# Seven block products in place of eight in the last two panels of an output projection

## The chip, the core and the metric

One core of a Trainium2 chip runs the whole kernel. The metric is the device time of one execution in microseconds (us); the time before is the median of three runs.

## The reference, cut to what matters

One layer of a decoder works on 512 prompt rows and 32 sample rows, 544 in all, of width 1024. After two gated branches come the output projection, a channel mixer and an embedding:

```python
merged = jax.nn.sigmoid(gate_a) * (a @ w_oa) + jax.nn.sigmoid(gate_b) * (b @ w_ob)
x = x + merged @ w_o
h2 = _rmsnorm(x, g_ffn)
x = x + jnp.square(jax.nn.relu(h2 @ w_ff1)) @ w_ff2
gate = jax.nn.sigmoid(_rmsnorm(x, g_ple) @ w_ple_gate)
x = x + gate * (pe @ w_ple_proj)
```

The change concerns `merged @ w_o`, a product of 544x1024 with 1024x1024 in float32.

## The kernel before, in words

**Precision.** Every float32 operand is split into a rounded part (`..._hi`, type fp32r, cast by ScalarE) and the rest (`..._lo`, a subtraction by VectorE). A product is three matmuls: hi with hi, hi with lo, lo with hi.

**Layout.** Activations lie transposed: 8 blocks of 128 features, each with 544 columns, used as two halves of 272. The merged activation is `mA`; half of it is split into `h_hi` and `h_lo`. The residual stream is `xT`.

**Panels and units.** Weights come in panels of 256 columns (512 KB in each of two loads), and each panel gives two units of 128 output features. In the first part of the kernel a *slot* is one unit; each engine's program is written out slot by slot, with its work for a slot in a fixed order (the loops over `SLOTS`, TensorE L1581, VectorE L2042, ScalarE L1078, GpSimd L2389). The projection is the kind `wo`, four panels, units 0 to 7, slots 96 to 103; the branch's `ob` ends in slot 95, and eight short units `pj` (the ple projection, 12 matmuls each) follow in slots 104 to 111. A `wo` unit is 48 matmuls: 8 blocks of the inner dimension, three matmuls, two halves (`block_unit`, L1336).

**What a `wo` slot does before.** ScalarE casts the next panel (`split_hi`, L749), evacuates the unit (`evacuate`, L825) and squares the new `xT` block for the norm (`square_x`, L924). VectorE splits the next panel (`split_lo`, L1704) and adds the unit to `xT` (`add_to_x`, L1959). GpSimd adds the square to `ss` (`add_square`, L2372). Slots 96 to 98 also take transposes of the ple input (`take_transposes`, L938). The SP queue loads each panel once the panel before it in the same buffer is split (`load_panel`, L621).

**Seven products.** The channel mixer already has panels (`seven`, L115) that multiply 2x2 blocks by seven products in place of eight. Weights and activation are cut in 2x2 blocks: the inner dimension into 512 and 512, the two units of the panel, and the two halves of the columns. A product (`product`, L1599) is 12 matmuls of 272 columns: 4 blocks, three matmuls. The order is p1, p2, p5, p6, p4, p3, p7 (`PRODUCTS`, L127). Four combinations of the activation are summed by VectorE (`combine`, L1768), cast by ScalarE (`combined_hi`, L1190) and subtracted by VectorE (`combined_lo`, L1781). The combinations of the weights are four in-place sums of 128x512 blocks by VectorE (`add_blocks`, L1731), each after the one before, then cast (`sums_hi`, L780) and split (`pair_lo`, L1717). A half-width block is split apart (`one_hi`, L772; `one_lo`, L1724). Four partial results are copied from the accumulator (`part`, L785) and added (`add_parts`, L1741). A panel has four counts of finished weight splits, which TensorE waits for before p1, p2, p5 and p6. Split weights lie in four places of 1024 columns, taken in turn; a cast waits for the last product that read the place (`pair_hi`, L762).

**The norm after the projection.** `ss` is complete after the eighth square; TensorE sums it after `pj` unit 3 (`norm_sum`, L1538), VectorE and GpSimd make the inverse root (`norm_mean`, L1962; `norm_inverse`, L2384), and TensorE spreads it inside the first unit of the channel mixer (`norm_spread`, L1545).

## Time and profile before

| what | value |
|---|---|
| time, median of 3 runs | 1044.94 us |
| lowest and highest run | 1041.84 and 1045.57 us |
| profiled execution: span | 1041.0 us |
| profiled execution: its own time outside the span | not given |
| TensorE matmuls, busy | 1023.5 us, 98% |
| VectorE busy | 774.4 us, 74% |
| ScalarE busy | 518.5 us, 50% |
| GpSimd busy | 245.6 us, 24% |
| projection `wo` in the trace | 547 to 596.7 us |

How to read it: the span runs from the first to the last instruction of one execution. The busy share of matmuls counts pipelined instructions whose ends are modelled. Times in the rows below are microseconds from the span's start; "PE" is TensorE, "PEld" its weight loads, "DVE" VectorE, "ACT" ScalarE, "POOL" GpSimd. In lists in order of time, a bracket gives the idle time of the engine before the instruction and what ended it.

### The profile page before, as it was taken

How to read it: one execution, taken by the hardware profiler on the slowest of the kernel's cores; microseconds unless marked ns; L12 is line 12 of the kernel's file. 1: busy time of each engine (PE TensorE's matmuls, PEld its weight loads, DVE VectorE, ACT ScalarE, POOL GpSimd, SP SyncE). 2: the span in 40 equal slices, each digit the busy share in tenths (PEclk: the TensorE clock that was granted, in tenths of full speed). 3: DMA queues.
4: the chain of work that ended last, by engine and by line, in shares of the span. 5: the costliest groups of instructions: out<-in, count | busy, mean ns of one | idle time of the engine just before them, and what ended most of it. 6: DMA issues, size and time to landing. Idle time of an engine off the chain costs nothing.

```text
span 1041.0 us, 20872 instructions
## 1 busy us (share of the span) xinstructions
PE 1023.5 (98%) x8310; PEld 1008.5 (97%) x8310; DVE 774.4 (74%) x1004; ACT 518.5 (50%) x1253; POOL 245.6 (24%) x381
## 2 busy tenths in 40 slices
PE   9999999999999999999999999999999999999997
PEld 7999999999999999999999989999999999999997
DVE  6679888988899878999674368747856875786553
ACT  6773797658845574352264385414522531453332
POOL 2441233122312003958201211100100100012300
PEclk9999999999999999999999999999999999999999
DMA  6557556776687765776843335655664574573412
GB/s 186 192 178 231 200 177 208 227 242 206 208 256 213 210 218 148 224 218 186 258 142 122 122 122 208 214 183 172 229 209 152 195 247 168 171 252 130 162 54 86
DMA packets 131634, 195.89 MB, mean 188 GB/s; under 512 B 32321, under 2 KB 109473, under 8 KB 129746
## 3 DMA queue, kind: packets, MB, share of 16 engines
q1 hardware_dynamic: 107616, 125.51, 37.9%
q0 software_dynamic: 10560, 63.28, 18.3%
q10 hardware_dynamic: 13362, 5.77, 2.0%
q8 instruction: 66, 1.08, 0.4%
q14 instruction: 30, 0.25, 0.1%
HBM read 185.55 MB, written 62.00 MB: 238 GB/s over the span
## 4 chain that ended last, share of the span: by engine, by line
PE 66%; DVE 13%; ACT 5%; issue 5%; DMA 5%; POOL 3%; SPq 3%; ACTq 0%; DVEq 0%; POOLq 0%
PE gm L1347 26%; PE gm L1603 7%; PE psSO L1603 4%; PE gm L1321 4%; PE gm L1322 3%; PE gm L1323 3%; PE psT L1603 3%; DMA w_raw<-in_w_in 3%; PE psSO L1651 2%; PE psSO L1347 2%; PE psT L1347 2%; PE psT L1651 2%; DVE w_lo L1708 2%; POOL kv L2363 2%; ACT prob L1123 2%
## 5 line engine op out<-in xcount | busy, mean ns | idle before, releaser
L1321 PE MATMUL gm<-w_hi,h_hi 128*128 128x256 f32 x640 | 186.9, 292 | 1.1 <-DVE w_lo L1708 0.9
L1322 PE MATMUL gm<-w_hi,h_lo 128*128 128x256 f32 x640 | 180.8, 282 | 0.0
L1323 PE MATMUL gm<-w_lo,h_hi 128*128 128x256 f32 x640 | 180.1, 281 | 0.0
L1347 PE MATMUL gm<-h_hi,w_hi 128*128 128x272 f32 x624 | 132.7, 294 | 0.4 <-ACT z L852 0.4
L1347 PE MATMUL gm<-h_hi,w_lo 128*128 128x272 f32 x624 | 130.0, 290 | 0.0
L1347 PE MATMUL gm<-h_lo,w_hi 128*128 128x272 f32 x624 | 129.4, 289 | 0.0
L1321 PEld LDWEIGHTS gm<-w_hi,h_hi 128*128 128x128 f32 x640 | 120.8, 189 | 3.1 <-issue 1.7
L1323 PEld LDWEIGHTS gm<-w_lo,h_hi 128*128 128x128 f32 x640 | 121.2, 189 | 0.0
L1322 PEld LDWEIGHTS gm<-w_hi,h_lo 128*128 128x128 f32 x640 | 120.6, 188 | 0.0
L2352 POOL DMA_DIRECT2D out_kvs<-in_cache_kv_w x64 | 35.0, 547 | 345.2 <-PE gm L1347 120.6
L1708 DVE TENSOR_TENSOR w_lo<-w_raw,w_hi 128x1024 fp32r<-128x1024 f32 x76 | 90.5, 1228 | 21.3 <-ACT w_hi L755 20.8
L1347 PEld LDWEIGHTS gm<-h_hi,w_hi 128*128 128x128 f32 x624 | 98.1, 190 | 1.5 <-ACT z L852 0.6
L1347 PEld LDWEIGHTS gm<-h_lo,w_hi 128*128 128x128 f32 x624 | 98.6, 190 | 0.0
L1347 PEld LDWEIGHTS gm<-h_hi,w_lo 128*128 128x128 f32 x624 | 98.2, 190 | 0.0
L755 ACT CAST w_hi<-w_raw 128x1024 fp32r<-128x1024 f32 x76 | 76.8, 1046 | 30.4 <-DMA w_raw<-in_w_in 16.5
L765 ACT CAST w_hi<-w_raw 128x1024 fp32r<-128x1024 f32 x49 | 50.2, 1048 | 82.6 <-PE psSO L1347 28.5
L1347 PE MATMUL gm<-x_hi,w_hi 128*128 128x272 f32 x384 | 80.4, 291 | 0.0
L1347 PE MATMUL gm<-x_hi,w_lo 128*128 128x272 f32 x384 | 79.6, 289 | 0.0
L1347 PE MATMUL gm<-x_lo,w_hi 128*128 128x272 f32 x384 | 79.3, 288 | 0.0
L2363 POOL DMA_DIRECT2D kv<-in_cache_kv_w x128 | 69.4, 708 | 32.8 <-DVE acc L1954 16.8
L1721 DVE TENSOR_TENSOR w_lo<-w_raw,w_hi 128x1024 fp32r<-128x1024 f32 x49 | 59.0, 1221 | 11.9 <-ACT w_hi L765 11.8
L1347 PEld LDWEIGHTS gm<-x_lo,w_hi 128*128 128x128 f32 x384 | 60.4, 189 | 0.0
(378 smaller groups left out, 2662.7 us busy)
## 6 DMA issues: line engine op xcount, KB each, us to landing
out_kvs<-in_cache_kv_w POOLq DMA_DIRECT2D x64, 510.0 KB, 4.7
w_raw<-in_w_in SPq DMA_DIRECT2D x60, 512.0 KB, 6.2
w_raw<-in_w_ff SPq DMA_DIRECT2D x36, 512.0 KB, 5.7
kv<-in_cache_kv_w SPq DMA_DIRECT2D x128, 128.0 KB
kv<-in_cache_kv_w SPq DMA_DIRECT2D x64, 256.0 KB
out_kvs<-in_cache_kv_w POOLq DMA_DIRECT2D x32, 508.0 KB, 5.3
w_more<-in_w_ff SPq DMA_DIRECT2D x26, 512.0 KB, 6.1
kv<-in_cache_kv_w POOLq DMA_DIRECT2D x128, 64.0 KB, 3.3
```

Source lines behind the costliest of these rows:

```text
L755: nc.scalar.copy(w_hi[:, r, hh * 1024:(hh + 1) * 1024], w_raw[:, hh]).then_inc(w_hi_done, 1)
L765: nc.scalar.copy(w_pair(w_hi, PAIRS[p] + n).rearrange("p (k n) -> p k n", k=4), raw(p, hh)).then_inc(w_hi_done, 1)
L1321: nc.tensor.matmul(out, lh, wh, start=k == 0, stop=False)
L1322: nc.tensor.matmul(out, ll, wh, start=False, stop=False)
L1323: last = nc.tensor.matmul(out, lh, wl, start=False, stop=k == KD - 1)
L1347: last = nc.tensor.matmul(pair[:, half, 0:HALF], w, x[:, k0 + k, half * HALF:(half + 1) * HALF], start=first, stop=end)
L1603: last = nc.tensor.matmul(bank[:, 0:HALF], w[wx][:, k], x[xx][:, k], start=start and k == 0 and wx == xx, stop=k == 3 and wx == 1, skip_gr ...
L1651: last = nc.tensor.matmul(banks(u + sub)[:, half, 0:HALF], w, x[:, k, half * HALF:(half + 1) * HALF], start=first, stop=end, skip_group_ch ...
L1708: vec.tensor_tensor(w_lo[:, r, cols], w_raw[:, hh], w_hi[:, r, cols].bitcast(F32), ALU.subtract).then_inc(w_lo_done, 1)
L1721: vec.tensor_tensor(w_pair(w_lo, x).rearrange("p (k n) -> p k n", k=4), raw(p, hh), w_pair(w_hi, x).rearrange("p (k n) -> p k n", k=4).bit ...
L2352: pool.dma_start(dst, src).then_inc(cache_copied, 16)
L2363: pool.dma_start(dst, src).then_inc(late_landed[n % RING], 16)
```

## The change

Panels 2 and 3 of `wo` (`MIXED`, units 4 to 7) become seven-product panels. Their activation combinations are taken from `mA`, in slots 96 to 98, beside units 0 to 2 (`combine_mixed` and `mixed_lo` on VectorE, `mixed_hi` on ScalarE, with the factor 0.5 in the last two). They lie in new tiles `tc_hi` and `tc_lo` over inputs of the earlier projections. Panel 2's weight sums are made in slots 98 and 99, panel 3's in slot 100; panel 3 is loaded into a new buffer `w_mixed` over the first part of `mA`, once the four sums are made. The units are added to `xT` by `add_to_mixed`. Panel 2 accumulates in `psT` and `psSO`, panel 3 in `gm`. The squares of units 4 to 7 go to `sqf`. Counts of semaphores of the channel mixer are shifted to match. `pair_free`, `product` and `seven_products` move up in the file. The first weights of the channel mixer are cast in `pj` slots 0 and 3, after the evacuation, where the first cast stood in the last `wo` slot. The diff, cut:

```diff
+MIXED = [PANELS.index(("wo", 0, i)) for i in (2, 3)]
+
+
 def seven(p):
 
     j, q = divmod(p - P_FF, FF_PANELS)
-    return P_FF <= p < P_PG and q < 4 and (j > 0 or q >= 2)
-
-
-SEVENS = [p for p in range(P_FF, P_PG) if seven(p)]
+    return p in MIXED or P_FF <= p < P_PG and q < 4 and (j > 0 or q >= 2)
+
+
+SEVENS = [p for p in range(P_PG) if seven(p)]
+
+
+def first_unit(p):
+
+    return UNIT["wo", 2 * PANELS[p][2]] if p in MIXED else U_FF + 2 * (p - P_FF)
...
     j, q = divmod(p - P_FF, FF_PANELS)
+    if p == MIXED[1]:
+        return 3
...
     p = P_FF + (u - U_FF) // 2
+    if u < U_FF:
+        return (2 if UNITS[u][0] == MIXED[0] else 0) + u % 2
...
+        w_mixed = sb("w_mixed", [128, 2, 1024], F32, A_QK1)
+        tc_hi = [sb(f"tc_hi{x}", [128, 4, HALF], F32R, A_QK + x * XB) for x in range(4)]
+        tc_lo = [sb(f"tc_lo{x}", [128, 4, HALF], F32R, A_V + x * XB) for x in range(4)]
+        wo_one_hi = sb("wo_one_hi", [128, 2, 512], F32R, A_R + 4 * NT * 4)
+        wo_one_lo = sb("wo_one_lo", [128, 2, 512], F32R, A_R + 4 * NT * 4 + 4096)
...
+                    w_mixed[:, hh].rearrange("p (k n) -> p k n", k=4))[raw_set(p)]
+
+        def one_place(p):
+
+            n = SEVENS.index(p) % 2
+            hi, lo = (wo_one_hi, wo_one_lo) if p in MIXED else (w_one_hi, w_one_lo)
+            return [x[:, n].rearrange("p (k n) -> p k n", k=4) for x in (hi, lo)]
 
         def w_pair(hi, n):
 
...
+                        sp.wait_ge(xc_summed, 8)
                     nk = 1024 // (256 if p >= P_FF else COLS.get(PANELS[p][0], 256))
-                    dst = raw(p, hh) if p >= P_FF else w_raw[:, hh].rearrange("p (k n) -> p k n", k=nk)
...
+                    act.wait_ge(ss_done, 4)
+                u = first_unit(p)
                 src = banks(u + 1)[:, 1, 0:HALF] if bank else banks(u)[:, 1, 0:HALF]
                 nc.scalar.copy(dst, src).then_inc(part_out, 1)
...
+            def mixed_hi(n):
+
+                x, src, scale = ((2, 0, 0.5), (0, 1, 0.5), (1, 1, -0.5), (3, 1, 0.5))[n]
+                act.wait_ge(xc_summed, n + 1)
+                nc.scalar.mul(tc_hi[x][:], xc_sum[src][:], scale).then_inc(xc_hi_done, 1)
+
+            def mixed_slot(s):
+
+                p = UNITS[s][0]
+                if s == first_unit(MIXED[0]):
+                    sums_hi(p, 0, 2)
+                    one_hi(p + 1)
+                    part(p, 0)
+                    raw_hi(p + 1, 1)
+                    part(p, 1)
+                    part(p, 2)
+                elif s == first_unit(MIXED[0]) + 1:
+                    sums_hi(p + 1, 1, 1)
+                    part(p, 3)
+                    square_x(4, 4, zc(UNIT["wo", 4]))
+                elif s == first_unit(MIXED[1]):
+                    sums_hi(p, 0, 2)
+                    square_x(5, 5, zc(UNIT["wo", 5]))
+                    part(p, 0)
+                    raw_hi(p + 1, 0)
+                    part(p, 1)
+                    part(p, 2)
+                else:
+                    raw_hi(p + 1, 1)
+                    part(p, 3)
+                    square_x(6, 6, zc(UNIT["wo", 6]))
+                    square_x(7, 7, zc(UNIT["wo", 7]))
 
             def gained_hi(n, m, zu):
...
                 p, kind, g, i, sub = UNITS[s]
+                if p in MIXED:
+                    mixed_slot(s)
+                    continue
...
+                    one_hi(MIXED[0])
+                    raw_hi(MIXED[0], 1)
+                    mixed_hi(3)
+                elif sub == 0 and not late_split(s) and kind != "pj":
                     split_hi(p + 1, (p + 1) % 2, panel_end(p - 1))
+                if s == UNIT["wo", 3]:
+                    sums_hi(MIXED[0], 1, 1)
                 if s - 1 in MERGED:
                     merged_hi(MERGED[s - 1])
+                if s == UNIT["wo", 0]:
+                    mixed_hi(0)
+                    mixed_hi(1)
+                if s == UNIT["wo", 1]:
+                    mixed_hi(2)
                 if s >= 1 and UNITS[s - 1][4] == 2 and UNITS[s - 1][1] == "v":
                     act.wait_ge(unit_out, s)
                 evacuate(s)
                 if late_split(s):
                     split_hi(p + 1, (p + 1) % 2, panel_end(p - 1) if p >= 1 else None)
-                if (kind, i, sub) == ("wo", 3, 1):
-                    half_hi(P_FF, 0)
-                if (kind, sub) == ("pj", 3):
-                    half_hi(P_FF, 1)
+                if kind == "pj" and sub in (0, 3):
+                    raw_hi(P_FF, sub // 3)
                 if kind == "pj":
                     if sub == 0:
-                        act.wait_ge(unit_ready, READY[UNIT["wo", 7]])
...
                         last = block_unit(r, n, 128 * sub, 2, b2, pT_hi, pT_lo, split=split)
+
+            def pair_free(u):
+
+                if UNITS[min(u, U_FF - 1)][0] == MIXED[0]:
+                    pe.wait_ge(o_out, len(PIECES))
+                    pe.wait_ge(t_out, TINDEX[("ps",)] + 1)
+                elif u < U_FF:
+                    pe.wait_ge(unit_out, u - 3)
+                elif pair_before(u) is not None:
+                    pe.wait_ge(unit_out, pair_before(u) + 1)
...
+                pair_free(u + 1)
+                product(p, "p1", B, one, x11, True)
+                pe.wait_ge(w_lo_done, SPLITS[p] + 2)
+                pair_free(u)
+                product(p, "p2", A, bd[0], x21, True)
+                pe.wait_ge(w_lo_done, SPLITS[p] + 3)
+                if n in (0, len(MIXED)):
+                    pe.wait_ge(xc_lo_done, 4 if n == 0 else 8)
+                product(p, "p5", C, yu[1], t1, True)
+                pe.wait_ge(w_lo_done, SPLITS[p] + 4)
+                pe.wait_ge(part_out, 4 * n + 1)
+                product(p, "p6", B, wv[0], t2, False)
+                product(p, "p4", Dd, bd[1], t4, True)
+                pe.wait_ge(part_out, 4 * n + 2)
+                product(p, "p3", C, yu[0], x22, False)
+                pe.wait_ge(part_out, 4 * n + 3)
+                product(p, "p7", B, wv[1], t3, False)
 
...
+                if UNITS[s][0] in MIXED:
+                    if UNITS[s][4] == 0:
+                        seven_products(UNITS[s][0])
+                    continue
...
                 j, uu = divmod(2 * (p - P_FF) + m, FF_UNITS)
-                if uu >= 2:
+                if p in MIXED:
+                    dve.wait_ge(z_used, zc(first_unit(p)) - 1 + (m if p == MIXED[1] else 0))
+                elif uu >= 2:
...
                 vec.tensor_tensor(x2_lo[:, uu], z[:, m], x2_hi[:, uu].bitcast(F32), ALU.subtract).then_inc(hid_lo, 1)
+
+            def add_to_mixed(p, m):
+
+                dve.wait_ge(unit_out, first_unit(p) + m + 1)
+                x = xT[:, 2 * PANELS[p][2] + m]
+                vec.tensor_tensor(x, x, z[:, m], (ALU.add, ALU.subtract)[m]).then_inc(z_used, 1)
+
+            def mixed_slot(s):
+
+                p = UNITS[s][0]
+                if s == first_unit(MIXED[0]):
+                    pair_lo(p, 0, 2)
+                    one_lo(p + 1)
+                    pair_lo(p + 1, 1, 0)
+                    for n in range(4):
+                        add_blocks(p + 1, n)
+                elif s == first_unit(MIXED[0]) + 1:
+                    add_parts(p, 0)
+                    pair_lo(p + 1, 1, 1)
+                    add_to_mixed(p, 0)
+                    add_parts(p, 1)
+                    add_to_mixed(p, 1)
+                elif s == first_unit(MIXED[1]):
+                    pair_lo(p, 0, 2)
+                    pair_lo(p + 1, 0, 0)
+                else:
+                    add_parts(p, 0)
+                    pair_lo(p + 1, 1, 1)
+                    add_to_mixed(p, 0)
+                    add_parts(p, 1)
+                    add_to_mixed(p, 1)
+
+            def combine_mixed(n):
+
+                first, second = slice(0, HALF), slice(HALF, NT)
+                top, low = mA[:, 0:4], mA[:, 4:8]
+                out, in0, in1, op = ((0, low[:, :, second], top[:, :, second], ALU.subtract),
+                                     (1, top[:, :, first], top[:, :, second], ALU.subtract),
+                                     (1, xc_sum[1][:], low[:, :, second], ALU.add),
+                                     (1, xc_sum[1][:], low[:, :, first], ALU.subtract))[n]
+                dve.wait_ge(z_used, zc(UNIT["ob", 7]))
+                if n >= 2:
+                    dve.wait_ge(xc_summed, n)
+                    dve.wait_ge(xc_hi_done, n)
+                vec.tensor_tensor(xc_sum[out][:], in0, in1, op).then_inc(xc_summed, 1)
+
+            def mixed_lo(n):
+
+                x, src, scale = ((2, 0, 0.5), (0, 1, 0.5), (1, 1, -0.5), (3, 1, 0.5))[n]
+                dve.wait_ge(xc_summed, n + 1)
+                dve.wait_ge(xc_hi_done, n + 1)
+                vec.scalar_tensor_tensor(out=tc_lo[x][:], in0=xc_sum[src][:], scalar=scale, in1=tc_hi[x][:].bitcast(F32), op0=ALU.mult,
+                                         op1=ALU.subtract).then_inc(xc_lo_done, 1)
 
             def combine(n):
...
+                if p in MIXED:
+                    mixed_slot(s)
+                    continue
...
-                if sub == 0 and not late_split(s) and kind != "pj":
+                if s == UNIT["wo", 2]:
+                    one_lo(MIXED[0])
+                    pair_lo(MIXED[0], 1, 0)
+                    mixed_lo(3)
+                    add_blocks(MIXED[0], 0)
+                    add_blocks(MIXED[0], 1)
+                elif sub == 0 and not late_split(s) and kind != "pj":
                     split_lo(p + 1, (p + 1) % 2)
+                if s == UNIT["wo", 3]:
+                    add_blocks(MIXED[0], 2)
+                    add_blocks(MIXED[0], 3)
+                    pair_lo(MIXED[0], 1, 1)
                 if kind == "pj" and sub in (0, 5):
-                    half_lo(P_FF, sub // 5)
+                    pair_lo(P_FF, sub // 5, sub // 5)
                 if s == 63:
...
+                if s == UNIT["wo", 0]:
+                    combine_mixed(0)
+                    combine_mixed(1)
+                    mixed_lo(0)
+                    mixed_lo(1)
+                if s == UNIT["wo", 1]:
+                    combine_mixed(2)
+                    mixed_lo(2)
+                    combine_mixed(3)
                 if kind == "ob":
                     m, r = 4 * i + sub, (zc(s) - 1) % 2
...
                     pool.wait_ge(ss_done, n)
-                    gp.tensor_tensor(ss[:], ss[:], sq[:, m % 2], ALU.add).then_inc(ss_done, 1)
+                    gp.tensor_tensor(ss[:], ss[:], (sqf if 4 <= n < KD else sq)[:, m % 2], ALU.add).then_inc(ss_done, 1)
 
...
```

## Rows read from the trace of the kernel before

**Rows 1.** The page: the span, and each engine's busy time.
```profile
span 1041.0 us, 20872 instructions
...
PE 1023.5 (98%) x8310; PEld 1008.5 (97%) x8310; DVE 774.4 (74%) x1004; ACT 518.5 (50%) x1253; POOL 245.6 (24%) x381
```

**Rows 2.** The chain of waits: start, us, engine, tile, line.
```profile
569.40 27.27 PE gm L1347 x216
...
612.97 1.13 PE psSO L1548 x2
...
719.01 10.57 PE gm L1603 x84
```

**Rows 3.** Windows: us, busy PE, PEld, DVE, ACT, POOL, clock, DMA.
```profile
572.00:584.00 12.00, 12.00 (x98) 12.00 (x97) 4.28 (x5) 4.44 (x6) 3.18 (x3) 1.00 0.41 141
```

**Rows 4.** Source lines: ns min/median/max, first and last start, shapes.
```profile
L1779 DVE TENSOR_TENSOR xc_sum<-x_gain,x_gain x1: 1293/1293/1293, 619.6 to 619.6; 128x1088 f32<-128x1088 f32 x1
...
L1196 ACT ACTIVATE xc_hi<-xc_sum x4: 1114/1114/1116, 620.9 to 637.1; 128x1088 fp32r<-128x1088 f32 x4
...
L1786 DVE SCALAR_TENSOR_TENSOR xc_lo<-xc_sum,xc_hi x4: 1282/1284/1292, 625.7 to 638.3; 128x1088 fp32r<-128x1088 f32 x4
...
L1739 DVE TENSOR_TENSOR w_raw<-w_raw x28: 682/691/694, 631.8 to 908.8; 128x512 f32<-128x512 f32 x28
...
L1721 DVE TENSOR_TENSOR w_lo<-w_raw,w_hi x49: 1212/1220/1227, 616.2 to 1012.4; 128x1024 fp32r<-128x1024 f32 x49
...
L765 ACT CAST w_hi<-w_raw x49: 1032/1050/1055, 611.9 to 1011.1; 128x1024 fp32r<-128x1024 f32 x49
```

**Rows 5.** Order of time: VectorE, then ScalarE, in the output projection.
```profile
548.75 2.36 DVE L1708 TENSOR_TENSOR w_lo<-w_raw,w_hi 128x1024 fp32r<-128x1024 f32 x2
551.03 0.72 DVE L2151 SCALAR_TENSOR_TENSOR h_lo<-mA,h_hi 128x544 fp32r<-128x544 f32 x1
554.00 0.72 DVE L1960 TENSOR_TENSOR xT<-xT,z 128x544 f32<-128x544 f32 x1 [2.25 <-ACT z L895]
...
572.63 0.61 ACT L895 COPY z<-gm 128x544 f32<-128x544 f32 x1 [2.87 <-PE gm L1347]
```

**Rows 6.** VectorE beside GpSimd: order of time, and one source line.
```profile
574.78 1.36 POOL L2382 TENSOR_TENSOR ss<-ss,sq 128x544 f32<-128x544 f32 x1 [3.96 <-ACT sq L929]
...
575.67 2.69 DVE L1708 TENSOR_TENSOR w_lo<-w_raw,w_hi 128x1024 fp32r<-128x1024 f32 x2 [1.53 <-ACT w_hi L755]
...
L1983 DVE SCALAR_TENSOR_TENSOR h_lo<-xT,gcol,h_hi x16: 761/779/1347, 601.2 to 982.6; 128x544 fp32r<-128x544 f32 x16
...
555.54 0.63 POOL L2379 COPY ss<-sq 128x544 f32<-128x544 f32 x1 [19.12 <-ACT sq L929]
...
944.39 0.72 DVE L1960 TENSOR_TENSOR xT<-xT,z 128x544 f32<-128x544 f32 x1
...
944.43 1.18 POOL L2379 COPY ss<-sq 128x544 f32<-128x544 f32 x1 [11.61 <-ACT sq L929]
```

**Rows 7.** Order of time: VectorE, GpSimd, ScalarE round the projection's end.
```profile
579.29 0.73 DVE L1960 TENSOR_TENSOR xT<-xT,z 128x544 f32<-128x544 f32 x1 [0.93 <-ACT z L895]
...
580.80 1.35 POOL L2382 TENSOR_TENSOR ss<-ss,sq 128x544 f32<-128x544 f32 x1 [4.18 <-ACT sq L929]
...
599.60 0.60 ACT L892 COPY proj<-gm 128x544 f32<-128x544 f32 x1
```

**Rows 8.** TensorE in order of time, and windows of 1 us.
```profile
513.18 1.05 PE L1464 MATMUL psT<-fold,acc 128*128 128x32 f32 x8 [1.52 <-DVE acc L2128]
...
515.00:516.00 1.00, 1.00 (x8) 1.00 (x7) 0.03 (x1) 0.00 (x0) 0.00 (x0) 0.64 0.78 307
516.00:517.00 1.00, 1.00 (x6) 1.00 (x6) 0.00 (x0) 0.00 (x0) 0.00 (x0) 0.50 1.07 340
...
518.00:519.00 1.00, 1.00 (x7) 1.00 (x7) 0.00 (x0) 0.12 (x1) 0.00 (x0) 0.65 1.00 293
...
600.25 0.52 PE L1347 MATMUL gm<-pT_hi,w_hi 128*128 128x272 f32 x2 [0.60 <-ACT proj L892]
```

More of the change, by code:

```diff
@@ L1386, in unit, with product @@
                         last = block_unit(r, n, 128 * sub, 2, b2, pT_hi, pT_lo, split=split)
+            def pair_free(u):
[6 more added lines that the diff above has]
+                    pe.wait_ge(unit_out, pair_before(u) + 1)
+            def product(p, name, bank, w, x, start):
+                for k in range(4):
+                    for wx, xx in ((0, 0), (0, 1), (1, 0)):
+                        last = nc.tensor.matmul(bank[:, 0:HALF], w[wx][:, k], x[xx][:, k], start=start and k == 0 and wx == xx,
+                                                stop=k == 3 and wx == 1, skip_group_check=True)
+                last.then_inc(unit_ready, 1)
@@ new lines, in seven_products @@
+            def seven_products(p):
+                n, u, s = SEVENS.index(p), first_unit(p), PAIRS[p]
+                (A, C), (Dd, B) = (banks(u)[:, 0], banks(u)[:, 1]), (banks(u + 1)[:, 0], banks(u + 1)[:, 1])
+                one = one_place(p)
+                bd, yu, wv = [[[block_of(w_pair(x, s + y), m) for x in (w_hi, w_lo)] for m in range(2)] for y in range(3)]
+                first, second = slice(0, HALF), slice(HALF, NT)
+                x11, x21, x22 = [[x[:, k:k + 4, cols] for x in (h_hi, h_lo)] for k, cols in ((0, first), (4, first), (4, second))]
+                t1, t2, t3, t4 = [[tc_hi[x], tc_lo[x]] if p in MIXED else [xc_hi[x], xc_lo[x]] for x in range(4)]
+                pe.wait_ge(w_lo_done, SPLITS[p] + 1)
+                pair_free(u + 1)
[15 more added lines that the diff above has]
+                product(p, "p7", B, wv[1], t3, False)
@@ L2029, in _ @@
                 tile_half_lo(0, half)
-                half_lo(0, half)
+                first_lo(half)
             tile_lo(1)
```

97 lines of the change are left out of this document (31 added, 66 removed).

## The prediction, made before the change was run

> **What bounds the kernel now.** I read the page first, for the engines' shares: TensorE is busy 98% of a span of 1041.0 us [rows 1], so only TensorE time counts, and other engines matter where TensorE waits for them. Next the chain of waits round the change: from 569.40 to 596.67 it is TensorE alone, then ScalarE and VectorE take most of it until the spread of the norm at 612.97, inside the first unit of the channel mixer [rows 2]. Then the windows: in the second half of the output projection VectorE and ScalarE are busy under 4.5 of 12 us [rows 3], so the change moves work to engines with room on average. Whether it is on time is a matter of order, so the last views are the lists in order of time.
>
> The profiled span stands 3.9 us below the median of 1044.94, and 0.8 below the fastest run. No view shows more of that execution than its span. The sum below is a difference; I carry it over to the median.
>
> **What is taken away.** A panel of two units has 96 matmuls, seven products of 12 have 84. In the channel mixer 84 of these take 10.57 us [rows 2], 0.126 each; 24 fewer are worth **3.0 us**. The casts, splits and evacuations that go with them were off the path.
>
> **What is added, and when it is done.** Four sums of the merged activation, four halved casts, four differences; per panel one half-width split, one more full split, four sums of weight blocks, four evacuated parts and two adds into z. All have like-shaped rows [rows 4]: 1.29 a sum, 1.11 a cast, 1.28 a difference, 0.69 a block sum, 1.22 and 1.05 a weight split on VectorE and ScalarE; the parts are half as wide as an evacuation, and an add is 0.73 [rows 7]. Between dependent instructions of two engines I put 0.04 us; one that follows on its own engine with no dependence starts 0.07 to 0.09 before the other ends. The starting point is unchanged: VectorE's last piece of h_lo at 551.03 [rows 5].
>
> Sums 0 and 1 then end at 552.95 and 554.16, ScalarE's casts at 554.10 and 555.31, the differences at 556.64. The add of unit 0 into xT starts at 556.6 where it was 554.00, and its evacuation, which now stands behind two casts, ends 2.0 us later. Nothing waits: unit 2 needs that bank at 559.7. The next slot, by the same steps, ends the fourth sum at 562.51; that frees the SP queue to load the last panel, 15 us before ScalarE wants it. Behind it in SP's queue stands the load of the ple projection, which waits for panel 2's last split, at 580.0 below, and is wanted some 10 us after. Behind GpSimd's adds stand copies of the cache, which no engine here waits for.
>
> In the third slot ScalarE does the half block (565.35), the other half (566.30), the fourth cast (567.33) and only then evacuates unit 2 (567.84, 1.1 late). VectorE follows with two splits, the last difference (568.78), two block sums (570.12), the add of unit 2 (570.76) and a split of pT (571.36). The transposes of the ple input are taken at 571.7, just before panel 2 needs their bank at 572.45.
>
> Then it gets late. VectorE has two block sums left. The square of unit 2 ends at 571.46, and GpSimd adds it. **A VectorE instruction with two SBUF inputs that meets such an add is held up**: a pair of splits that meets 0.47 us of it takes 2.69 [rows 6], not 2.36 [rows 5], and of 16 pieces of h_lo one takes 1.35 where the median is 0.78 [rows 6]. The other way round GpSimd waits: its copy takes 1.18 where VectorE was first, 0.63 alone [rows 6]. So the third block sum holds GpSimd off until 571.97, the fourth waits for GpSimd and ends at 573.8 in place of 572.7. By the Trainium skill (SBUF — State Buffer, Who interferes with whom) this is an exclusive lock, held for the whole instruction, and the loser blocks. The pair lost 0.33 of its 0.47, and I take 0.14 off each overlap; by the full overlap the total below would be some 0.5 us higher.
>
> ScalarE casts the first summed block from 573.84 to 574.89, then evacuates unit 3 (575.4; PE had ended it at 572.45). VectorE splits that block until 576.15 and adds unit 3 to xT until 576.80; ScalarE squares it (577.5) and casts the second summed block until 578.45. VectorE's split of that meets 0.44 us of GpSimd's add and ends at 580.0.
>
> TensorE in panel 2: p1 and p2 run 572.45 to 575.46. p5 needs the split of 576.15: **0.74 us lost**. p6 needs that of 580.0: **2.36 lost**. p4, p3 and p7 follow to 586.08.
>
> Panel 3: its first sums end at 584.54 and the split for p5 at 586.9, early. The add of unit 4 ends at 587.53, that of unit 5 gets the port first and holds GpSimd's add of square 4 back to 588.9 to 590.15. The second sum's split, ready at 589.2, meets this and ends at 591.25, when p6 has waited since 590.6: **0.7 lost**. p7 ends at **597.3**, where the last unit ended about 596.5.
>
> The ple projection: before, its first evacuation starts at 599.60 [rows 7], after an evacuation, an add, a square and a cast. Now ScalarE has square 6 and square 7 in front. The add of unit 6 ends at 598.34; GpSimd's add of its square starts 1.51 us after that add's start (579.29 to 580.80 in [rows 7]), at 599.12, and VectorE's add of unit 7, two dependent instructions after the same start, at 599.13. If GpSimd is first, unit 7 ends at 600.9, if VectorE is, at 599.85. The bounds are 0 and 1.1 us; I take GpSimd, by the 0.01 that the rows give it. Square 7 ends at 601.6, the first evacuation at 602.1; the cast of the mixer's first weights, which stood ahead of it, now stands behind, and costs TensorE's second pair of banks 0.3. From there the order of before leads to the spread of the norm at 615.2, where it was 612.97 [rows 2].
>
> **Sum:** -3.0 for matmuls, +3.8 for three waits, +1.4 before the norm: **+2.2 us**, 1047.1. Of the 1.4, 1.1 hang on the near tie. Later panels only shift: they keep the order of their queues, the weights' buffers and the count of sums.
>
> Bounds of what no row shows: whether the block sums meet GpSimd's adds. Never: 1.1 less in panel 2, 0.7 in panel 3, 1.1 at the tie, which leaves -0.7, 1044.2. Fully, by overlap: +2.7, 1047.6.
>
> **Rivals.**
> *The cover holds.* If evacuation and square of unit 3 come a microsecond or two earlier than my twenty-step chain, p5 and p6 wait under 0.5 us each, and the tie falls to VectorE: -3.0, +1.0 for waits, +0.3: 1043.2, or 1042.3 with no waits at all. For it: VectorE and ScalarE have over 7 of 12 us free [rows 3]. Against: each step waits for the other engine, so the free time can't be used.
> *The clock falls.* After 511.4 TensorE idled 1.52 us and ran eight narrow transposing matmuls, and the granted clock went to 0.50, its lower level of 1.2 GHz, from about 515 to 519 [rows 8]. Lost there, by four windows of 1 us, the middle two alike: 0.36 + 0.50 + 0.50 + 0.35 = 1.7 us. Panel 2's waits of 0.74 and 2.36 us, with one product between them, are like it: +1.7, 1048.8. Against: 0.60 us of idleness in the ple projection left the matmuls after it at full pace [rows 8]. The Trainium skill (TensorE: Matmul & The Clock Gate, What's actually happening) says "the default state is throttled, and activity releases the throttle"; by that rule the long wait would count against the change, while here one stretch shows it.
> *Slower by more than 0.5%.* The same fall, but lasting, because p6 of panel 3 and the ple projection wait too. At 1.2 GHz work takes twice its time; it decides once 24 matmuls (3.0 us at full clock) more than forecast have run at the lower level, 6 us of it against 3.5 in [rows 8]. At 7.5 us: +2.2 +3.8, 1050.9. Against: at half clock the products are long enough for the splits to be on time, so the waits that would hold it down vanish.
> *The change does less than it says*: no sign; the products are the same helper as in the mixer.
>
> **How the numbers follow.** Forecast (1045.5 to 1048.2) 0.43; cover holds 0.24 (1042.3 to 1044.5); clock falls 0.22; lasting fall 0.09; anything else 0.02. A measurement of this kernel can tell about 0.5%, 5.2 us: 1039.7 to 1050.2. The removed work is 3.0 us, so faster by more needs a low median besides (runs of before differ by 3.7): 0.03. Slower: the lasting fall, and a clock fall on a high median: 0.11. Same: 0.86. The range takes the cover's 1042.3 less 0.5 and the clock's 1048.8 plus 1.0.
>
> **What would show it.** 24 fewer matmuls in the projection's panels; TensorE waits for w_lo before p5 and p6 of panel 2 (0.7 and 2.4) and p6 of panel 3 (0.7); VectorE's block sums and splits stretched beside ss adds; the first proj evacuation some 2 us later; granted clock 1.00 from 572 to 600. If p6 waits under 1 us, or the span of the projection shrinks by 2 us or more, my chain is wrong; a clock of 0.5 there speaks for the third case.

## The result, and the profile after

Run beside each other, the changed kernel took 1045.55 us (median of 22 runs) and the kernel before 1042.60 (22 runs): ratio 1.0026, 95% interval 1.0013 to 1.0038, so 2.7 us slower (1.4 to 4.0). A second series of 7 runs gave 1.0043 (1.0028 to 1.0059), 4.5 us. Both ratios lie within the 0.5% that the prediction called no change, on the slower side.

The first part of the profile's page after:

```profile
span 1043.1 us, 20886 instructions
...
PE 1021.9 (98%) x8286; PEld 1006.0 (96%) x8286; DVE 798.4 (77%) x1028; ACT 525.8 (50%) x1265; POOL 245.6 (24%) x381
```

Against [rows 1] TensorE has the 24 matmuls fewer and 1.6 us less to do, and the span is 2.1 us longer. VectorE has 24.0 us more, ScalarE 7.3: they are still far from full. The loss must be waits, so the list to read is TensorE in order of time, with the idle time and its releaser in brackets at the end:

```profile
574.09 0.40 PE L1474 MATMUL psT<-tc_hi,w_hi 128*128 128x272 f32 x1 [0.55 <-DVE w_lo L1801]
577.91 0.60 PE L1474 MATMUL psSO<-tc_hi,w_hi 128*128 128x272 f32 x1 [2.05 <-DVE w_lo L1801]
...
590.43 0.39 PE L1474 MATMUL gm<-tc_hi,w_hi 128*128 128x272 f32 x1 [0.25 <-DVE w_lo L1801]
598.67 0.52 PE L1419 MATMUL gm<-pT_hi,w_hi 128*128 128x272 f32 x2 [0.41 <-DVE z L1833]
...
601.70 0.52 PE L1419 MATMUL gm<-pT_hi,w_hi 128*128 128x272 f32 x2 [1.26 <-ACT proj L917]
603.80 0.52 PE L1419 MATMUL gm<-pT_hi,w_hi 128*128 128x272 f32 x2 [0.34 <-ACT proj L917]
...
615.03 1.12 PE L1666 MATMUL psSO<-sqf,ones 128*128 128x512 f32 x2 [0.80 <-DVE sqf L2105]
```

The first three are p5 and p6 of the first of the two panels and p6 of the second, waiting for VectorE's half of a weight split; the next three are the ple projection. Before, the same stretch had one such wait, 0.60 us in the ple projection [rows 8], beside the 0.80 at the spread of the norm, which both kernels have:

```profile
596.49 0.41 PE L1347 MATMUL gm<-pT_hi,w_hi 128*128 128x272 f32 x2
...
612.97 1.13 PE L1548 MATMUL psSO<-sqf,ones 128*128 128x512 f32 x2 [0.80 <-DVE sqf L1971]
```

The window that was full of TensorE work before [rows 3] reads after the change:

```profile
572.00:584.00 12.00, 9.40 (x62) 8.96 (x61) 8.03 (x10) 6.45 (x10) 1.79 (x2) 0.86 0.51 173
```

Two numbers in it: TensorE idle for 2.6 of 12 us, and a granted clock of 0.86.

**How to compare these profiles.** The profile after can't be set beside that of before by its clock time: its last piece of h_lo, up to which the two kernels do the same work, starts at 548.93, where it was 551.03 [rows 5].

```profile
548.93 0.71 DVE L2298 SCALAR_TENSOR_TENSOR h_lo<-mA,h_hi 128x544 fp32r<-128x544 f32 x1
```

So I cut every profile of this study, those of the experiments below included, at two events that all kernels have: the start of that piece of h_lo, and TensorE's start of the spread of the norm (612.97 before [rows 2]). The stage between them holds the whole change. Medians and ratios are from the timed runs, the other columns from the one profiled execution of each kernel, in us:

| kernel | median, ratio to before in its series | h_lo | spread | stage | spread to end |
|---|---|---|---|---|---|
| before | 1042.60 | 551.03 | 612.97 | 61.94 | 428.0 |
| less24 | 1038.88, 0.9963 | 549.75 | 608.72 | 58.97 | 428.2 |
| changed | 1045.55, 1.0026 | 548.93 | 615.03 | 66.10 | 428.1 |
| after_again | 1046.24, 1.0043 | 550.18 | 615.09 | 64.91 | 428.0 |
| filled_wait | 1046.32, 1.0031 | 551.81 | 616.76 | 64.95 | 428.0 |
| early_splits | 1045.13, 1.0017 | 556.34 | 620.46 | 64.12 | 428.0 |
| short_gpsimd | 1042.09, 0.9990 | 550.79 | 612.54 | 61.75 | 428.0 |
| squares_behind | 1043.64, 1.0017 | 545.88 | 609.59 | 63.71 | 428.0 |
| early_parts | 1042.31, 1.0003 | 549.51 | 612.31 | 62.80 | 428.0 |
| early_parts_and_squares | 1040.75, 0.9989 | 548.04 | 609.62 | 61.58 | 428.0 |
| all_parts_first | 1042.62, 1.0003 | 559.39 | 620.60 | 61.21 | 428.0 |
| all_parts_short_gpsimd | 1040.79, 0.9983 | 549.58 | 609.99 | 60.41 | 428.2 |
| both_again | 1042.55, 0.9993 | 552.23 | 613.79 | 61.56 | 428.2 |
| all_parts_again | 1041.23, 0.9984 | 556.11 | 616.92 | 60.81 | 428.1 |

The last column is the same in all fourteen to 0.2 us: whatever the stage loses, the end loses, and nothing is given back or lost behind it. The h_lo column differs by 13.5 us between executions, for reasons ahead of the change (in the profile of early_splits, for instance, TensorE waited 4.25 us for a tile of an earlier stage). Single spans are no measure here; the stage is, to some tenths of a us. It says: the changed kernel needs **3.0 us more** (64.91 and 64.95 against 61.94), or 4.2 in the execution in which the clock fell.

**Where the stage grew.** TensorE's first matmul of the ple projection, at 596.49 before, splits it in two. For the changed kernel I read its second profiled execution (after_again), in which the clock did not fall:

```profile
550.18 0.72 DVE L2298 SCALAR_TENSOR_TENSOR h_lo<-mA,h_hi 128x544 fp32r<-128x544 f32 x1
...
574.51 0.28 PE L1474 MATMUL psT<-h_hi,w_lo 128*128 128x272 f32 x1
575.34 0.39 PE L1474 MATMUL psT<-tc_hi,w_hi 128*128 128x272 f32 x1 [0.55 <-DVE w_lo L1801]
575.57 0.29 PE L1474 MATMUL psT<-tc_lo,w_hi 128*128 128x272 f32 x1
...
579.18 0.39 PE L1474 MATMUL psSO<-tc_hi,w_hi 128*128 128x272 f32 x1 [2.06 <-DVE w_lo L1801]
...
590.49 0.39 PE L1474 MATMUL gm<-tc_hi,w_hi 128*128 128x272 f32 x1 [0.48 <-DVE w_lo L1801]
...
596.63 0.42 PE L1419 MATMUL gm<-pT_hi,w_hi 128*128 128x272 f32 x2
...
598.73 0.52 PE L1419 MATMUL gm<-pT_hi,w_hi 128*128 128x272 f32 x2 [0.41 <-DVE z L1833]
...
601.76 0.52 PE L1419 MATMUL gm<-pT_hi,w_hi 128*128 128x272 f32 x2 [1.26 <-ACT proj L917]
...
603.86 0.52 PE L1419 MATMUL gm<-pT_hi,w_hi 128*128 128x272 f32 x2 [0.32 <-ACT proj L917]
...
615.09 1.13 PE L1666 MATMUL psSO<-sqf,ones 128*128 128x512 f32 x2 [0.81 <-DVE sqf L2105]
```

From h_lo to the ple projection: 46.45 us, 45.5 before, so +1.0. From there to the spread: 18.46 against 16.5, so +2.0. A wait costs more than the bracket says. The bracket counts from the modelled end of the matmul before (574.51 + 0.28), but at full pace the next one would have started 0.126 after its start, 0.15 earlier; and the second matmul after the wait follows 0.23 us behind the first (575.34 to 575.57), not 0.126. With that 0.25 added the three waits for splits cost 0.80 + 2.31 + 0.73 = 3.84 us, and 24 matmuls fewer give back 3.0.

### The profile page after: what moved, and what is told of

It is laid out like the page before. It is cut to its first block, busy times and chain, and to the rows that moved or that the text cites. A ratio compares the mean times of both kernels' runs of the same rounds, so it can differ in the third digit from the quotient of the medians.

```text
span 1043.1 us, 20886 instructions
## 1 busy us (share of the span) xinstructions
PE 1021.9 (98%) x8286; PEld 1006.0 (96%) x8286; DVE 798.4 (77%) x1028; ACT 525.8 (50%) x1265; POOL 245.6 (24%) x381
## 4 chain that ended last, share of the span: by engine, by line
PE 64%; DVE 16%; ACT 7%; issue 5%; POOL 3%; DMA 3%; SPq 1%; ACTq 0%; DVEq 0%; POOLq 0%
PE gm L1419 21%; PE gm L1474 8%; PE psSO L1474 5%; PE gm L1393 4%; PE gm L1394 4%; PE gm L1395 4%; PE psT L1474 3%; PE psSO L1732 2%; PE psT L1419 2%; PE psSO L1419 2%; PE psT L1732 2%; DVE w_lo L1789 2%; POOL kv L2519 2%; DVE kv L2082 2%; ACT prob L1195 2%
## 5 line engine op out<-in xcount | busy, mean ns | idle before, releaser
L1419 PE MATMUL gm<-h_hi,w_hi 128*128 128x272 f32 x560 | 119.4, 295 | 0.3 <-DVE w_lo L1789 0.2
L1419 PE MATMUL gm<-h_hi,w_lo 128*128 128x272 f32 x560 | 116.1, 289 | 0.0
L1419 PE MATMUL gm<-h_lo,w_hi 128*128 128x272 f32 x560 | 116.0, 289 | 0.0
L1789 DVE TENSOR_TENSOR w_lo<-w_raw,w_hi 128x1024 fp32r<-128x1024 f32 x70 | 82.6, 1219 | 13.0 <-ACT w_hi L783 12.7
L1419 PEld LDWEIGHTS gm<-h_hi,w_hi 128*128 128x128 f32 x560 | 88.0, 189 | 1.4 <-issue 0.9
L1419 PEld LDWEIGHTS gm<-h_lo,w_hi 128*128 128x128 f32 x560 | 88.5, 189 | 0.0
L1419 PEld LDWEIGHTS gm<-h_hi,w_lo 128*128 128x128 f32 x560 | 87.9, 190 | 0.0
L1801 DVE TENSOR_TENSOR w_lo<-w_raw,w_hi 128x1024 fp32r<-128x1024 f32 x56 | 69.0, 1247 | 16.7 <-ACT w_hi L788 16.6
```

The costliest lines, as they stand in the source:

```text
L1419: last = nc.tensor.matmul(pair[:, half, 0:HALF], w, x[:, k0 + k, half * HALF:(half + 1) * HALF], start=first, stop=end)
L1789: vec.tensor_tensor(w_lo[:, r, cols], w_raw[:, hh], w_hi[:, r, cols].bitcast(F32), ALU.subtract).then_inc(w_lo_done, 1)
L1801: vec.tensor_tensor(w_pair(w_lo, x).rearrange("p (k n) -> p k n", k=4), raw(p, hh), w_pair(w_hi, x).rearrange("p (k n) -> p k n", k=4).bit ...
```

## The experiments

**1. Only the removed work.** The kernel before with half the contraction left out of the last output block: 24 matmuls fewer, nothing added.

```diff
-last = block_unit(r, n, 128 * sub, KD, b2, h_hi, h_lo, 0, wk, u, split)
+last = block_unit(r, n, 128 * sub, KD if (i, sub) != (3, 1) else 4, b2, h_hi, h_lo, 0, wk, u, split)
```

> The kernel before, with 24 matmuls less: the last output block of the projection leaves out the second half of its inner dimension. It prices the removed work alone, with no wait added. Forecast's theory: TensorE bounds this stage, so 24 x 0.125 = 3.0 us faster than before (ratio 0.997). Rival: something beside TensorE sets the end of the stage (the evacuation and the norm's chain after it), then under 1 us faster. 24 matmuls fewer than before in either case.

Measured: ratio 0.9963 (0.9948 to 0.9978), 3.9 us faster (2.3 to 5.4); the stage is 58.97, shorter by 2.97. The price of the removed work, 3.0 us, is right, and the changed kernel therefore adds 6 us of stage time to get it.

**2. The long wait filled.** In the changed kernel, 16 matmuls whose result is thrown away stand between p5 and p6 of the first of the two panels.

```diff
                 product(p, "p5", C, yu[1], t1, True)
+                if p == MIXED[0]:
+                    pe.wait_ge(unit_out, UNIT["wo", 2] + 1)
+                    for _ in range(16):
+                        nc.tensor.matmul(gm[:, 0, 0:HALF], bd[0][0][:, 0], x21[0][:, 0], start=True, stop=True, skip_group_check=True)
```

> The changed kernel, with 16 extra matmuls (2.0 us) into a free accumulator between p5 and p6 of panel 2, where TensorE idles 2.05 us in the changed profile; the lateness stays, only the idleness goes. If the idleness makes the granted clock fall and that costs 1.6 us, the clock reads 1.00 from 572 to 600 and the kernel is some 1.6 us faster than the changed one, +1.1 against before. Rival, the waits alone explain the loss and the fall costs nothing or comes anyway: as slow as the changed kernel, +2.7 against before.

Measured: ratio 1.0031 (1.0014 to 1.0048), stage 64.95. Its list of TensorE:

```profile
578.61 2.18 PE L1500 MATMUL gm<-h_hi,w_hi 128*128 128x272 f32 x16
580.84 0.40 PE L1474 MATMUL psSO<-tc_hi,w_hi 128*128 128x272 f32 x1
```

The filler takes the place of the wait, and p6 starts 29.03 us after h_lo, where it does 29.00 without the filler (579.18 - 550.18 above). So the wait is idle time that TensorE can do nothing about: it is set by VectorE's split. The clock was 1.00 throughout, and the time is not better than the changed kernel's: the rival came. So the fall of the clock does not show as a steady part of the loss, though these intervals alone would not exclude its 1.2 us. The next point shows why.

**3. The same kernel again.** No edit.

> The changed kernel once more, beside the three that follow on the same chip. It repeats its 2.7 us (1.4 to 4.0) over the kernel before. If it comes out under 1 us, differences between kernels of this size can only be read within one series of runs.

Measured: ratio 1.0043 (1.0028 to 1.0059; 7 runs): slower again, but by 4.5 us, above the 1.4 to 4.0 that were expected. The kernel before had its lowest median of all series here (1041.67), so differences of this size in the times hold within a series only; the stage of 64.91 is the better measure. Windows of 2 us after p6's wait, first of the first execution, then of this one (the third number from the right is the granted clock):

```profile
576.00:578.00 2.00, 0.09 (x1) 0.09 (x1) 1.67 (x2) 1.95 (x4) 1.24 (x2) 0.94 0.33 98
578.00:580.00 2.00, 2.00 (x9) 2.00 (x10) 1.97 (x3) 0.48 (x2) 0.00 (x0) 0.50 0.65 202
580.00:582.00 2.00, 2.00 (x14) 2.00 (x14) 1.90 (x4) 0.39 (x1) 0.00 (x0) 0.71 0.92 317
```

```profile
578.00:580.00 2.00, 0.82 (x6) 0.82 (x7) 2.00 (x3) 1.69 (x4) 0.51 (x2) 1.00 0.70 245
580.00:582.00 2.00, 2.00 (x18) 2.00 (x17) 1.93 (x3) 0.39 (x1) 0.00 (x0) 1.00 0.44 133
```

With the same two waits (0.55 and 2.05 or 2.06) the clock fell to its lower level of 1.2 GHz in one execution and stayed at 2.4 GHz in the other; it stayed there too in squares_behind, whose waits were 0.56 and 2.05. The fall cost the stage 66.10 - 64.91 = 1.2 us where it came: p6 and p4 took 4.58 us (577.91 to 582.49) in place of 3.12, and 0.2 came back because p6 of the second panel then waited 0.25 and not 0.48.

**4. GpSimd's adds made short.** In the changed kernel GpSimd adds only 32 of 544 columns of the squares of units 2 to 7, so that it hardly meets VectorE.

```diff
-gp.tensor_tensor(ss[:], ss[:], (sqf if 4 <= n < KD else sq)[:, m % 2], ALU.add)
+w = 32 if 2 <= n < KD else NT
+gp.tensor_tensor(ss[:, 0:w], ss[:, 0:w], (sqf if 4 <= n < KD else sq)[:, m % 2, 0:w], ALU.add)
```

> The changed kernel, but GpSimd's adds of the squares of units 2 to 7 take 32 of the 544 columns (the rest of those sums is left out). It takes away the meeting of GpSimd with VectorE. Forecast's theory: block sums back from 2.44 to 1.41 a pair, the split before p6 from 1.53 to 1.22, the last add from 1.81 to 0.72; the wait before p5 goes, that before p6 falls from 2.05 to about 0.8, too short for the clock to fall; in all 4 us faster than the changed kernel, about 1 us faster than before. Rival, the lateness is the chain's own length: p6 still waits over 1.5 us and under 1.5 us is won.

Measured: 1042.09 us, ratio 0.9990 (0.9973 to 1.0006), stage 61.75: 3.2 us shorter than the changed kernel's. No other single edit to the changed kernel gained as much, and this one moves no instruction. First the changed kernel's VectorE and GpSimd where they meet, in order of time, then the same block sums, and p6's wait, with short adds:

```profile
569.25 2.44 DVE L1818 TENSOR_TENSOR w_raw<-w_raw 128x512 f32<-128x512 f32 x2
...
569.50 1.65 POOL L2538 TENSOR_TENSOR ss<-ss,sq 128x544 f32<-128x544 f32 x1 [6.17 <-ACT sq L956]
...
575.45 1.33 POOL L2538 TENSOR_TENSOR ss<-ss,sq 128x544 f32<-128x544 f32 x1 [3.84 <-ACT sq L956]
...
576.33 1.53 DVE L1801 TENSOR_TENSOR w_lo<-w_raw,w_hi 128x1024 fp32r<-128x1024 f32 x1 [1.52 <-ACT w_hi L788]
...
587.46 4.13 POOL L2538 TENSOR_TENSOR ss<-ss,sqf 128x544 f32<-128x544 f32 x2 [10.22 <-ACT sqf L956]
...
588.34 2.04 DVE L1801 TENSOR_TENSOR w_lo<-w_mixed,w_hi 128x1024 fp32r<-128x1024 f32 x1 [0.27 <-ACT w_hi L788]
...
598.53 1.35 POOL L2538 TENSOR_TENSOR ss<-ss,sqf 128x544 f32<-128x544 f32 x1 [6.47 <-ACT sqf L956]
...
598.65 1.81 DVE L1853 TENSOR_TENSOR xT<-xT,z 128x544 f32<-128x544 f32 x1
```

```profile
571.11 1.41 DVE L1818 TENSOR_TENSOR w_raw<-w_raw 128x512 f32<-128x512 f32 x2
...
578.45 0.39 PE L1474 MATMUL psSO<-tc_hi,w_hi 128*128 128x272 f32 x1 [1.54 <-DVE w_lo L1801]
```

Two block sums take 2.44 us beside GpSimd and 1.41 without; the split for p6 1.53 in place of 1.22; that of the second panel 2.04; the add of unit 7, 1.81 in place of 0.72. With short adds p5's wait and the second panel's are gone, and the ple projection loses 1.1 us less. But p6 of the first panel still waits 1.54, where about 0.8 was expected: p5 no longer waits, so TensorE is at p6 sooner. This part is the chain itself, split behind cast behind evacuation. Contention made p6 1.3 us late (it starts 27.66 us after h_lo, not 29.00): 0.8 of that stood as p5's wait, half a us in p6's.

**5. The splits earlier.** The changed kernel with the first panel's block sums, and the cast and split for p6 of each panel, moved ahead of the evacuation, add and square they stood behind.

```diff
                 if s == UNIT["wo", 3]:
                     sums_hi(MIXED[0], 1, 1)
+                    sums_hi(MIXED[0], 0, 2)
...
                 if s == first_unit(MIXED[0]):
-                    sums_hi(p, 0, 2)
                     one_hi(p + 1)
                     part(p, 0)
...
                     sums_hi(p + 1, 1, 1)
+                    sums_hi(p + 1, 0, 2)
                     part(p, 3)
...
                 elif s == first_unit(MIXED[1]):
-                    sums_hi(p, 0, 2)
                     square_x(5, 5, zc(UNIT["wo", 5]))
```

(VectorE's queue is changed alike, the two bank waits of the first panel are parted, and its first part waits for three of GpSimd's adds, not four.)

> The changed kernel, with the same work in another order: panel 2's four block sums ahead of unit 2's add on VectorE, both casts of summed blocks ahead of unit 3's evacuation on ScalarE and both splits ahead of its add; likewise the second cast and split of panel 3 ahead of square and add of unit 4; waits for a free buffer of parts and banks made no wider than needed. Forecast's theory (the waits come from the order of the two queues): the waits before p5 and p6 (0.55, 2.05, 0.25) fall to under 0.3 together, the clock stays at 1.00, 4 us faster than the changed kernel, 1 to 2 us faster than before. Rival, the added work or the port is too much in any order: waits of 1 us or more remain and it stays slower than before.

Measured: ratio 1.0017 (0.9997 to 1.0038), stage 64.12, only 0.8 us better where 4 was expected. All waits for w_lo in the stage are gone; in their place stand 1.57 us before p6 of the first panel and 0.89 before that of the second. ScalarE and TensorE:

```profile
582.61 0.66 ACT L956 ACTIVATE sq<-xT 128x544 f32<-128x544 f32 x1 [1.60 <-DVE xT L2095]
583.18 0.60 ACT L803 CAST wo_one_hi<-w_mixed 128x512 fp32r<-128x512 f32 x1
583.68 0.38 ACT L821 COPY sq<-psSO 128x272 f32<-128x272 f32 x1
...
584.21 0.36 PE L1476 MATMUL psSO<-tc_hi,w_hi 128*128 128x272 f32 x1 [1.57 <-ACT sq L821]
```

p6 adds into the bank of p1, so it also waits until ScalarE has copied p1's part out of it (L821). That copy stood behind the square of unit 3, before which ScalarE stood idle for 1.60 us, waiting for VectorE's add into xT. A wait that had been covered by a longer one came out.

**6. The parts earlier as well.** Early splits, and the first part of each panel ahead of the square that stood before it.

```diff
                     one_hi(p + 1)
-                    part(p, 0)
...
+                    part(p, 0)
                     square_x(5, 5, zc(UNIT["wo", 5]))
-                    part(p, 0)
...
+                    if m == 3:
+                        part(MIXED[0], 0)
                     square_x(m, m, zc(u))
```

> The early splits once more, but ScalarE evacuates the first part of each of the two panels ahead of the square that stood before it (that of unit 3, and that of unit 5). My theory: the waits of 1.57 and 0.9 us that the early splits put in place of the late ones came from these two squares alone; with them gone panel 2 and panel 3 run with under 0.5 us of waits in all and no fall of the clock, which is 2.9 us of waits less than in the changed kernel: 2.5 to 4.5 us faster than it, so 2 us faster than the kernel before to no different. Rival: GpSimd's adds meet other VectorE work wherever it is put, so about as much comes back as a wait for w_lo or for the add into z in a later place; then 0 to 1 us faster than the changed kernel.

Measured: ratio 1.0003 (0.9990 to 1.0015), stage 62.80, 2.1 us shorter than the changed kernel's where 2.5 to 4.5 was expected. The first panel runs without waits; the second keeps one, of the two panels' waits that were expected to come to under 0.5 in all:

```profile
587.73 0.36 PE L1477 MATMUL gm<-tc_hi,w_hi 128*128 128x272 f32 x1 [1.04 <-ACT sq L821]
```

The part now stood behind the square of unit 4, which waits for an add just as that of unit 5 did. Clearing the one square was not enough.

**7. Two squares behind the first evacuation of the ple projection.** The changed kernel, and in the next run both edits together.

```diff
                     part(p, 3)
-                    square_x(6, 6, zc(UNIT["wo", 6]))
-                    square_x(7, 7, zc(UNIT["wo", 7]))
...
+                if kind == "pj" and sub == 0:
+                    square_x(6, 6, zc(UNIT["wo", 6]))
+                    square_x(7, 7, zc(UNIT["wo", 7]))
                 if kind == "pj" and sub in (0, 3):
                     raw_hi(P_FF, sub // 3)
```

(The evacuation now waits itself for VectorE's sums into z, which the squares ahead of it had waited for.)

> The changed kernel, with the squares of units 6 and 7 on ScalarE moved behind the first evacuation of the ple projection; nothing else moves. If those two squares (and GpSimd's add that holds up VectorE's add of unit 7) are what is late there, TensorE's wait of 1.26 us for that evacuation goes and the kernel is 1.0 to 1.6 us faster than the changed one. Rival: the evacuation's delay is only passed on to the sum of squares before the norm, since GpSimd adds those two squares later; then TensorE waits there instead and the time is that of the changed kernel within 0.5 us.

> Both together: early splits with early parts, and the squares of units 6 and 7 behind the first evacuation of the ple projection. If the waits were all that stood against the 3.0 us of removed matmuls, this is 3.5 to 5.5 us faster than the changed kernel and 1 to 3 us faster than the kernel before (ratio 0.997 to 0.999). If what is gained in one place is given back in the next, it is no better than the better of the two parts alone.

Measured: alone, ratio 1.0017 (1.0003 to 1.0031), stage 63.71, 1.2 us shorter than the changed kernel's; the waits of 1.26 and 0.34 for the evacuation are now one of 0.62, and nothing comes back at the norm:

```profile
594.42 0.73 DVE L1855 TENSOR_TENSOR xT<-xT,z 128x544 f32<-128x544 f32 x1
...
595.75 3.88 POOL L2540 TENSOR_TENSOR ss<-ss,sqf 128x544 f32<-128x544 f32 x2 [7.92 <-ACT sqf L957]
...
598.35 0.52 PE L1421 MATMUL gm<-pT_hi,w_hi 128*128 128x272 f32 x2 [0.62 <-ACT proj L918]
```

VectorE's add of unit 7 takes 0.73 here, since GpSimd now comes after it. Both edits together: ratio 0.9989 (0.9976 to 1.0002), stage 61.58: 62.80 less the same 1.2. The gains add up; the stage is now 0.4 us shorter than before, less than the 1 to 3 us expected.

**8. The last square out of the way, and what contention is left.** The first part of the second panel goes ahead of the square of unit 4 too; and the same with GpSimd's short adds.

```diff
                     part(p, 3)
+                    part(p + 1, 0)
                     square_x(4, 4, zc(UNIT["wo", 4]))
...
-                    part(p, 0)
                     square_x(5, 5, zc(UNIT["wo", 5]))
```

> The last version with one more step: ScalarE evacuates the first part of the last panel ahead of the square of unit 4 too, not only ahead of that of unit 5. My theory: the wait of 1.05 us before p6 of that panel came from this square, which stood waiting for VectorE's add while the product was long done; without it the stage is 1.2 to 1.3 us shorter (the wait and its restart), so 0.5 to 3 us faster than the kernel before (ratio 0.997 to 0.9995), with waits left only in the ple projection (0.4 and 0.6). Rival: GpSimd's adds, now a little later, hold up VectorE's adds and splits instead; the time is then that of the last version within 0.5 us.

> The same with GpSimd's adds of the squares of units 2 to 7 on 32 of 544 columns, so the sum of squares lacks most columns: what contention still costs in this order. If the order has taken all of VectorE's late work out of the path, nothing is gained: the same within 0.6 us. If VectorE is still held up on the path, it is 1 to 3 us faster, as the shortened adds made the changed kernel 3.7 us faster.

Measured: ratio 1.0003 (0.9986 to 1.0021), stage 61.21, only 0.4 us shorter where 1.2 was expected. The wait of 1.05 is gone; 0.27 came back at p3 of the second panel, whose own part now stands behind the square of unit 5 and a cast, and in this execution the ple projection waited 1.01 instead of 0.64 (a cast waited for a weight's DMA). With short adds: ratio 0.9983 (0.9964 to 1.0003), stage 60.41. GpSimd costs this order 0.4 to 0.8 us where it cost the changed kernel 3.2.

**9. The two best orders once more, side by side.**

> The version with early splits, early parts and the two squares behind the first evacuation, once more. Its stage, from VectorE's last piece of h_lo to the spread of the norm, took 61.58 us where the kernel before took 61.94, so by the stage it is 0.4 us faster than the kernel before: ratio 0.9985 to 1.0005. If its 0.9989 of the first series was the whole of a larger gain (1 us or more), this comes out at 0.999 or lower again.

> The version with the first part of the last panel ahead of the square of unit 4, once more and now beside the version without that step. By the stage (61.21 us against 61.58) it should be 0.4 us faster than that version and 0.7 faster than the kernel before: ratio 0.998 to 1.0002. If its 1.0003 of the first series stands, the step gains nothing in the time, and what the stage gains is inside the spread of single runs.

Measured: 0.9993 (0.9979 to 1.0007) and 0.9984 (0.9964 to 1.0005), stages 61.56 and 60.81. Every reading of both is a shorter stage than before, by 0.4 and by 0.7 to 1.1 us, and no interval of the times excludes "no change". By the stage, the best order found turns the loss of 3 us into a gain of about 1, a third of what the removed matmuls are worth; as a time it can't be told from the kernel before.

## Why the prediction was right, and where its sizes were off

The likeliest case came: +2.2 us forecast, +2.7 (1.4 to 4.0) measured, 1045.55 as the median where 1047.1 was given, beside 1042.60 for the kernel before, which had been 1044.94 in the runs shown. The base was 2.3 us too high, so 1045.55 stands at the very edge of the likeliest case's band (1045.5 to 1048.2); as a difference, +0.6 to +3.3, the band holds 2.7 well. Each run takes some 1.9 us longer than its span (1044.97 and 1043.1 in the first profiled execution of the changed kernel), so the span of 1041.0 stood for some 1042.9. The stage is the finer test: +2.2 forecast, +3.0 measured where the clock stayed up.

*Removed work.* -3.0 forecast, -2.97 in less24.

*The three waits.* 0.74, 2.36 and 0.7 forecast; 0.80, 2.31 and 0.73 measured in the second execution, restart included. The chain of some twenty steps held: p6's split was to end at 580.0 on the clock of before, and 576.33 + 1.53 + 2.1 (the shift of h_lo) is 579.96.

*The meetings with GpSimd* came where they were forecast, in the forecast order: the block sums first and GpSimd held off (its add took 1.65, not 1.36 as in [rows 6]), then VectorE held up. The rule taken from [rows 6], overlap less 0.14, can be tried on two rows above: the split met GpSimd for 575.45 + 1.33 - 576.33 = 0.45 us and lost 0.31; the add of unit 7 met it for 1.23 and lost 1.09. The Trainium skill (SBUF — State Buffer, Who interferes with whom) has the loser blocked while the other holds the lock; the trace agrees, but for 0.14 us of each overlap.

*The near tie* at unit 7 went to GpSimd by 0.12 us, as forecast by 0.01. That the order of two engines decided 1.1 us was right; the 0.01 was luck, and squares_behind shows the add at 0.73 where GpSimd comes after it.

*Price of GpSimd.* Between "never" and the forecast stood 2.9 us; short_gpsimd gave 3.2 of stage: 1.3 in the first panel, 0.7 in the second and 1.1 in the ple projection, where 1.1, 0.7 and 1.1 were forecast.

*The step that was mis-sized* is "+1.4 before the norm": the stretch from the ple projection to the spread grew by 2.0. Its two parts were 1.1 for the first evacuation and 0.3 for the second pair of banks. The first evacuation was to end at 602.1; it ended at

```profile
601.12 0.59 ACT L917 COPY proj<-gm 128x544 f32<-128x544 f32 x1
```

601.71, which is 602.56 on the clock of before (0.85 later), 0.46 behind the forecast: TensorE's third unit starts 5.13 us after the first (596.63 to 601.76), where it was 3.76 (596.49 to 600.25 [rows 8]), +1.4. The second part was counted by its idle time alone: 0.32 measured, but from the third unit to the spread the kernel needs 13.33 us in place of 12.72, +0.6. The chain also left out one wait, TensorE's second unit for VectorE's sum of unit 7's parts into z (0.41 in the list). It added nothing here, since the third unit had to wait for the evacuation in any case.

*The cover holds* (0.24): it did not. The splits were late by the forecast amounts. (Its 1042.3 without waits adds up to 1042.2.) VectorE and ScalarE had the free time on average that this rival named, and early_parts shows that it can be used, but only by another order.

*The clock falls* (0.22): half. In the first execution it did, right after p6's wait and to the level named, and cost 1.2 us of the stage against 1.7 forecast; matmuls at the lower level started 0.227 apart and not 0.126, 1.8 times and not twice as the next rival had it; in the second, and in squares_behind, the same waits left it at 1.00. The Trainium skill (TensorE: Matmul & The Clock Gate, What's actually happening) lets the long wait count against the clock; by these three executions the wait alone does not settle it. Since filled_wait had no fall and was no faster, I put no steady share of the 2.7 us on it. How often it falls is not measured: a timed run shows no windows.

*Slower by more than 0.5%, and does less than it says*: neither; the clock was back after 582, and the 24 matmuls are gone (8286 against 8310).

## What to carry to other kernels

Work moved to engines with free time costs nothing only if every step on the chain to the bottleneck is done in time. Write out the queues in order, and count for each instruction what the one ahead of it waits for: here three squares, waiting for an add, held back copies that were ready. When a wait is removed, look for the next one that it covered. And where executions differ by more than the change, cut the profiles at two events that both kernels have: the same kernel's stage came back within 0.4 us (61.58 and 61.56, 61.21 and 60.81, 64.91 and, with the wait filled, 64.95) wherever the clock stayed up, while the spans of the fourteen executions differed by over 11.

## What was not expected of the hardware

A wait of TensorE cost about 0.25 us more than its idle time: 0.15 before the first matmul, since the one before it is 0.28 long at a pace of 0.126, and 0.10 after it (575.34 to 575.57). The three waits for splits cost 0.75 us more this way than their brackets say.

The clock after a wait of 2.05 us fell in one execution out of three with that wait, all else in the stage alike. The stretch of [rows 8], ahead of the change, goes either way too. In the fourteen profiles the same eight narrow matmuls come after 0.81 to 1.87 us of idleness, and behind them the clock fell in ten and stayed at 1.00 in four: it stayed after 1.49 us in early_parts and fell after 1.28 in short_gpsimd. The length of the wait alone does not decide it.

VectorE holds up even a small add of GpSimd: in short_gpsimd the add of 32 columns took 0.55 us while two block sums ran, and 0.25 alone. The two block sums took their 1.41 all the same.

```profile
571.36 0.55 POOL L2539 TENSOR_TENSOR ss<-ss,sq 128x32 f32<-128x32 f32 x1 [6.17 <-ACT sq L956]
...
576.28 0.25 POOL L2539 TENSOR_TENSOR ss<-ss,sq 128x32 f32<-128x32 f32 x1 [3.90 <-ACT sq L956]
```
